# Two-block transformer on one core: SBUF areas placed a multiple of 256 bytes from the weight buffers

## What is computed

```python
def first_block(x, c, ctx, c_ctx, mod_w, mod_b, norm_g, ffn_w13, ffn_w2, conv_..., attn_..., ...):
    for i in range(DEPTH):                                   # DEPTH = 2; layer 0: conv, layer 1: attention
        mod = silu(c) @ mod_w[i] + mod_b[i]                  # shifts, scales, gates; modc from c_ctx
        lat = lat + 0.5 * gate * swiglu(modulate(lat, ...), ffn_w13[i, 0], ffn_w2[i, 0])   # hidden 2816
        lat = lat + gate * mixer(modulate(lat, ...))         # cx (256 context tokens) likewise
        lat = lat + 0.5 * gate * swiglu(modulate(lat, ...), ffn_w13[i, 1], ffn_w2[i, 1])

def second_block(x, mem, ...):
    for l in range(DEPTH):
        x = x + head_group_mixer(rmsnorm(x, mix_norm[l]), w_in[l], sb_norm[l], ret_norm[l], w_out[l])
        x = x + memory_cross_attn(rmsnorm(x, xa_norm[l]), rmsnorm(mem, mem_norm[l]), xa_wq[l], xa_wkv[l], xa_wo[l])
        x = x + peer_ffn(rmsnorm(x, peer_norm[l]), peer_wq[l], peer_keys[l], peer_u[l], peer_v[l])
    return rmsnorm(x, final_norm)
```

## Time and profile before

| | |
|---|---|
| median of three runs | 4156.93 us |
| profiled execution, its own time | 4151.06 us |
| its span, first to last instruction | 4149.2 us |
| granted TensorE clock, mean over the span | 0.969 |
| PE busy | 3906.5 us (94%) |
| PEld busy | 3415.6 us (82%) |
| DVE busy | 2833.6 us (68%) |
| ACT busy | 1606.6 us (39%) |
| POOL busy | 620.3 us (15%) |

### The profile page before, as it was taken

The page is one execution under the profiler, slowest core; times in us unless marked ns, Lnnn a source line. Parts: engine busy times, 40 slices in busy tenths (PEclk is TensorE's granted clock), DMA queues, the critical chain, the costliest instruction groups (busy, mean ns, idle before and its releaser), DMA issues.

```text
span 4149.2 us, 67374 instructions
## 1 busy us (share of the span) xinstructions
PE 3906.5 (94%) x23004; PEld 3415.6 (82%) x23004; DVE 2833.6 (68%) x4694; ACT 1606.6 (39%) x2218; POOL 620.3 (15%) x244
## 2 busy tenths in 40 slices
PE   7999999999999959998899999999888899999998
PEld 7888777887878739987899999888777899998886
DVE  6867667676843455637468887888445497888887
ACT  2223322223222334454444444333454444443333
POOL 0000000000000000055567000000246591000000
PEclk9999999999999989999999999999899999999998
DMA  6544434453532304553346565666533356556665
GB/s 225 170 156 147 154 106 147 137 180 109 191 108 85 113 10 133 186 188 115 105 155 204 191 194 193 233 235 238 188 109 138 112 190 202 193 192 220 235 234 183
DMA packets 203569, 685.37 MB, mean 165 GB/s; under 512 B 22528, under 2 KB 24704, under 8 KB 193920
## 3 DMA queue, kind: packets, MB, share of 16 engines
q1 hardware_dynamic: 174592, 573.45, 41.9%
q10 hardware_dynamic: 28800, 109.59, 7.3%
HBM read 646.25 MB, written 36.70 MB: 165 GB/s over the span
## 4 chain that ended last, share of the span: by engine, by line
PE 73%; issue 12%; POOL 10%; DVE 3%; ACT 1%; POOLq 0%; DMA 0%; SPq 0%; DVEq 0%; ACTq 0%
PE bank L532 23%; PE bank L533 23%; PE bank L534 22%; POOL low L499 10%; PE bank L940 1%; PE bank L939 1%; PE bank L579 1%; DVE qk_squares L1625 0%; PE bank L724 0%; PE bank L682 0%; DVE low L1390 0%; PE bank L698 0%; DVE h L1369 0%; ACT high L1004 0%; DMA mod_raw<-in_mod_w 0%
## 5 line engine op out<-in xcount | busy, mean ns | idle before, releaser
L1004 ACT ACTIVATE high<-raw 128x1024 fp32r<-128x1024 f32 x1044 | 1100.3, 1058 | 1266.3 <-PE bank L534 998.2
L532 PE MATMUL bank<-h_lo,high 128*128 128x256 f32 (+1 forms) x4432 | 1416.9, 320 | 52.5 <-DVE h_lo L1562 18.3
L533 PE MATMUL bank<-h_hi,high 128*128 128x256 f32 (+1 forms) x4432 | 1402.3, 316 | 0.0
L534 PE MATMUL bank<-h_hi,low 128*128 128x256 f32 (+1 forms) x4432 | 1401.5, 316 | 0.0
L1390 DVE TENSOR_TENSOR low<-raw,high 128x1024 fp32r<-128x1024 f32 x808 | 972.1, 1220 | 148.1 <-ACT high L1004 146.1
L499 POOL TENSOR_TENSOR low<-raw,high 128x1024 fp32r<-128x1024 f32 x240 | 620.1, 2600 | 2817.1 <-ACT high L1004 2816.7
L532 PEld LDWEIGHTS bank<-h_lo,high 128*128 128x128 f32 x4432 | 851.8, 192 | 118.7 <-issue 28.3
L533 PEld LDWEIGHTS bank<-h_hi,high 128*128 128x128 f32 x4432 | 852.2, 192 | 58.7
L534 PEld LDWEIGHTS bank<-h_hi,low 128*128 128x128 f32 x4432 | 850.4, 192 | 58.7
L532 PE MATMUL bank<-low,weighed_hi 128*128 128x512 f32 x1024 | 405.5, 396 | 0.0
L534 PE MATMUL bank<-high,weighed_lo 128*128 128x512 f32 x1024 | 405.0, 396 | 0.0
(11 more groups left out here) (266 smaller groups left out, 4441.2 us busy)
## 6 DMA issues: line engine op xcount, KB each, us to landing
raw<-in_experts SPq DMA_DIRECT2D x516, 512.0 KB, 3.3
raw<-in_w SPq DMA_DIRECT2D x176, 512.0 KB, 4.1
late_raw<-in_mod_late ACTq DMA_DIRECT2D x64, 1024.0 KB, 4.8
acts_spill<-acts_out ACTq DMA_DIRECT2D x128, 256.0 KB, 3.8
acts_in<-acts_spill SPq DMA_DIRECT2D x128, 256.0 KB, 3.4
raw<-in_w_in SPq DMA_DIRECT2D x56, 512.0 KB, 3.2
raw<-in_w SPq DMA_DIRECT2D x64, 384.0 KB, 3.2
raw<-in_w SPq DMA_DIRECT2D x64, 320.0 KB, 3.5
```

What stands on the lines that cost most here:

```text
L532: pe.matmul(out, a[0], b[1], start=start, stop=False, **more)
L533: pe.matmul(out, a[0], b[0], start=False, stop=False, **more)
L534: return pe.matmul(out, a[1], b[0], start=False, stop=stop, **more)
L1004: act.activation(high[:, slot * UNIT:(slot + 1) * UNIT], raw[:, slot * UNIT:(slot + 1) * UNIT], ACT.Copy)\
```

## The change

`rms` gets 16 columns for 8, and the region's start is rounded up to a multiple of 256 bytes from the start of `raw`. The first area then begins 56576 bytes (221 x 256) behind `raw`. The area of `h2_hi`, `h2_lo` and `late_raw` begins 8 columns (32 bytes) later than the end of `HOT`, and the areas behind it 64 columns (256 bytes) later than its end without these 8. No instruction is added or taken out, and on each of the five queues they stand in the same order as before.

| bytes from `raw`, modulo 256 | before | after |
|---|---|---|
| `raw`, `high`, `low`, `picked`, `gates_of`, `consts` | 0 | 0 |
| `hot_rows`, `hot_gated`, `weighed*`, `cond_rows`, `mem_lo` | 32 | 0 |
| `h2_hi`, `h2_lo`, `late_raw` | 32 | 32 |
| `acts_out`, `acts_in`, `mem_hi`, arena | 32 | 0 |

```diff
+        raw_at = (nc.sbuf_base + 31) // 32 * 32
         raw = sb("raw", SLOTS * UNIT)
...
-        rms = sb("rms", 8)
+        rms = sb("rms", 16)
...
-        region = (nc.sbuf_base + 31) // 32 * 32
+        region = raw_at + (nc.sbuf_base - raw_at + 255) // 256 * 256
...
-        HOT, H2, ACTS = 7 * SPREAD * P, KD * TOK, 8 * TOK
+        HOT, H2, ACTS, AHEAD = 7 * SPREAD * P, KD * TOK, 8 * TOK, 8
         hot_area = Area(0, HOT)
-        h2_area = Area(HOT, 2 * H2)
-        acts_area = Area(HOT + 2 * H2, ACTS)
-        arena_at, arena_cols = HOT + 2 * H2 + ACTS, NK * TOK
+        h2_area = Area(HOT + AHEAD, 2 * H2)
+        acts_at = HOT + 2 * H2 + 64
+        acts_area = Area(acts_at, ACTS)
+        arena_at, arena_cols = acts_at + ACTS, NK * TOK
...
-        h2_area = Area(HOT, 2 * H2)
+        h2_area = Area(HOT + AHEAD, 2 * H2)
...
-        mem_hi = Area(HOT + 2 * H2, ACTS).take("mem_hi", KD * TOK, f32r, k=KD)
+        mem_hi = Area(acts_at, ACTS).take("mem_hi", KD * TOK, f32r, k=KD)
```

## The result

The changed kernel takes 4104.02 us (median of 4 runs, 4103.55 to 4109.59) beside 4156.75 us for the kernel before: ratio 0.9875, 95% interval 0.9863 to 0.9888. The forecast was 4157 us, the range 4108 to 4190; both are wrong.

What follows compares the result with a forecast made beforehand. PE was taken as the bound, its time being matmuls times the distance between starts. All terms summed to 0 against the profiled 4151.06 us, carried over to the median as 4157 us; range 4108 to 4190.

Steps and rivals of the forecast that it cites:

- What bounds the kernel: Long stretches where PE never stops: time is the number of matmuls times the distance between starts, 233.0 ns for 512 columns.
- (1): Instructions on all queues: none added, removed or reordered, with the same shapes, semaphores and DMA sizes; 0 us.
- (5): VectorE: 256 sums of products go to relation 32, at most 1.8 us, hidden beside PE; 48 splits of h2, 0.3 us.
- (6): DMAs: starts of spilled and loaded tiles move by 224, 256 or 480 bytes, PE waits for none; 0 us.
- (2): 2944 groups of three 512-column matmuls go from relation 32 to 0: taken as 0, bounds +29 to -177 us.
- (3): 1072 groups of three 256-column matmuls go to relation 0: taken as 0, bounds +5 to -16 us.
- (4): 2752 groups of three 256-column matmuls on h2 keep relation 32: 0 us, a slow stretch perhaps 1 us.
- the phase gain: Relation 0 rids PE's streams of small slips, 1.0 to 1.4%, 24 to 34 us: about 4128 us; chance 0.26.
- The surcharge goes: The 20 ns extra per 512-column matmul vanish: up to 193 us gained, 3964 us; chance 0.10.
- The collision rival: At relation 0 load and stream collide, putting PE in its slower phase: 29 + 5 us more, 4192 us; chance 0.20.

Runs made afterwards that it cites:

- the bare series: Groups of 36 matmuls on PE alone, not the transformer, with varied columns and places: f32r with 512 columns took 226.7 ns at place 0, 233.3 at 32.
- the entry series: Matmuls on PE alone, not the transformer, behind differing first matmuls: 256 columns at 192 took 113.3 ns (9 times) or 117.8 (7).

## Why the prediction was wrong

- *What bounds the kernel*: right. The time is a number of matmuls times the distance between starts; the three terms of the result add up to the profiled difference within 2 us.
- *(1), (5), (6), instructions, VectorE, DMAs*: right. The 256 sums of products stay at 1224 ns, where 1231 was allowed, and the bare series has the transformer's paces with the other engines at rest. One reading in (5) was wrong: `hot_gated` from `gates_of` was to cost 1226 ns because of relation 32, but it still takes 1226 ns after the change, at relation 0.
- *(2), the wide triples at relation 0*: this is the step that failed. The term was put at 0 and is -20 ns a triple, -58.9 us, inside the bounds given (+29 to -177). Three reasons had been put for 0. That the two orders have the same 233 ns: they were two relations of a table in which nine of sixteen places lie at 233 to 235 ns and only two at 226.7. That the surcharge grows with the columns and not with the loads: 48 cycles at 512 and 24 at 256 are proportional at 32 by coincidence (384 columns have 32 there); at 0 they are 32 and 32, at 192 48 and 16. That hot against hot, the nearest row at relation 0, shows no hindrance: with 128 columns the load sets the pace, 111.6 ns at all four places tried, so this row could not have shown one.
- *(3), the narrow triples that move*: priced at 0 with +5 ns as upper bound; they cost +10 ns, 10.7 us. The bound was taken from the other paces seen in the same rows, not from the table's worst.
- *(4), `h2` untouched*: "0, or 1 us". It lost 1.7 ns a triple, 4.7 us. The relation stayed, but more of the stretches ran in the slower pattern; it did so too in the run that moved only the first area (351.8 ns). That their start chose it is carried over from the entry series, not tested in the transformer by itself. The 554 against 559 of the earlier trace rows were this effect: the prediction called it a phase effect that holds while PE does not stop, which the entry series confirms, and then did not ask what the change does to the phase.
- *The rivals*: the phase gain had the place right and gave 4128 us; the wide triples alone gave 2.9% where it allowed 1.0 to 1.4%, so it is mis-sized by more than two. "The surcharge goes" rested on a collision of stream and load that comes of the 32 bytes: one third of it went, not all. The collision rival was right for the narrow triples, at twice its price, and wrong for the wide ones. Its deciding point was 703 ns; it is 680.
- *The pages.* "SBUF — State Buffer" of the Trainium skill says in "Who interferes with whom" that PE never waits on anyone. No run here shows PE waiting for another engine, but PE's pace depends on where its streamed and its loaded tile stand against each other, and the zero that follows from the sentence is 52.7 us off. The 215.7 ns that the Trainium skill gives for 512 columns ("TensorE: Matmul & The Clock Gate", section "Wait — 56ns, not 53.3ns?") is what the bf16 groups show, 215.8; it is not the f32r pace at any place that was tried.
- *The range* was cut at 4108 by leaving out the large gain and shortening the other. With the bound of (2) at -177 and only plausible reasons for its 0, it should have reached far below 4108.

What stays open: the mechanism below the table. Shown are the dependence on the relation modulo 256, on the columns and on the start, for f32r and not for bf16 or plain float32; that most of the surcharge goes with a fixed stream; that fewer loaded columns shift it, down for 256 streamed columns at relation 0 and up for 512. Which accesses meet was not settled: neither the own nor the next weights explain the mixed places.

## What to carry to other kernels

Where PE never stops, divide the length of a stretch by its matmuls and compare with columns / 2.4 GHz; if f32r leaves a surcharge, place the streamed and the loaded tiles relative to each other and try several places modulo 256 bytes in a bare series, for each number of columns apart. A place with one steady pattern, or with patterns close to each other, is safer than one whose best is a matter of the start. Look at the granted clock of a bare series before comparing its groups. And a row in which something else sets the pace says nothing about a contention.

## What the runs showed that was not expected

- An f32r matmul of 512 columns takes 226.7 to 240.0 ns from start to start (the last 20 bytes off), one of 256 columns 113.3 to 122.7, by nothing but the place of its operands against each other.
- The same stretch of code can run in two steady patterns, 340.0 and 353.3 ns a triple at 192, until PE is interrupted; part of the difference between two executions of one kernel may come from this, which was not tested.
- f32r loads of 128, 64 and 32 columns set a floor of 111.7, 58.3 and 32.1 ns a matmul at granted clock 1.00 (the last two with 64 columns streamed).
- A stream that reads one column again and again runs at 218.7 ns for 512, with or without fixed weights.
